# Query up-projection placed behind the scores and gating products, and the last weight slice's low part ahead of a unit's work, in a one-layer hybrid decoder

## The chip, the cores and the metric

The kernel runs on one core of one Trainium2 chip. The metric is the device time of one execution in microseconds (us); lower is better. Five engines work side by side and meet at semaphores: TensorE (PE for matmuls, PEld for its weight loads), VectorE (DVE), ScalarE (ACT), GpSimd (POOL) and SyncE (SP, which issues most DMAs here).

## What is computed

One decoder layer over 1024 positions of width 1024, float32. Three sub-layers, each `x <- LayerNorm(alpha * x + f(x))`: a hybrid token mixer, a cross-attention into 256 memory tokens, and a mixture of 16 experts. The change touches only the front of the mixer:

```python
rq, rk, rv, rg, su, sv, cq, ckv, kr = jnp.split(x @ w_in, split_points, axis=-1)
rq, rk = apply_rope(rq), apply_rope(rk)              # retention, 4 heads of 64
ret = head_group_norm(retention_chunkwise(rq, rk, rv))
ret = jax.nn.silu(rg) * ret
sgu = spatial_gating(su, layer_norm(sv), sgu_w, sgu_b)   # per 128 positions
q  = (rms_norm(cq, q_norm_g) @ w_uq)                 # 256 -> 8 heads of 64 + 32
kv = (rms_norm(ckv, kv_norm_g) @ w_ukv)              # 128 -> 8 heads of 64 + 64
```

In the chunkwise retention each chunk of 128 positions needs its own scores (keys times queries, times a decay mask), a product of the queries with a running state, and an update of that state by the chunk's keys and values.

## The kernel before

The program is a row of phases with a barrier between them: `project`, `prepare`, `attend`, `mix_out`, `cross_attend`, `experts`, `overflow`. Within a phase each engine runs its own instruction list in the order in which the code is written; nothing reorders it across engines.

**`project`** computes `x @ w_in` in 32 units: four column chunks (in the order QK, LAT, UV, VG) times eight token tiles of 128. For precision both operands are split into a high and a low part, so each of the eight slices (`KD`, 128 rows of the contraction) costs three matmuls (L261 high times high, L262 high times low weights, L263 low times high weights); a unit is 24 matmuls into one of four PSUM banks. The weights of a chunk are kept in eight slices: ACT copies the high part of a slice (`whi`, L212), DVE subtracts to get the low part (`wlo`, L293). The buffers are single, so a slice of the next chunk may be written only when PE is through with the old one: `slice_free` lets slices 0 to 6 go when the last unit of the chunk has used them, and slice 7 when that unit is summed. `next_slices` places the splits in the lists of ACT and DVE: seven before the last unit's own work, the eighth at the head of the following unit, thus behind the last unit's own work.

```python
            c = u // NT
            if u % NT == NT - 1 and c < 3:
                for s in range(KD - 1):
                    split_w(c + 1, s)
            elif c and u % NT == 0:
                split_w(c, KD - 1)
```

PE waits for `wlo` slice by slice in the first unit of a chunk. DVE's own work for a unit is, for UV units, the layer norm of `sv` (L379 to L386, with a round trip to POOL), for LAT units the rotated key and the scaled latents, for VG units one product `sg` (L390). `unit_taken` counts units whose bank DVE has finished with; PE reuses a bank four units later. When all 32 low slices are made, SP issues six loads for the next phase (`w_uq`, `w_ukv`, `sgu_wT` and three small ones, L198 to L203); DVE scales them in `prepare_weights` ahead of the fourth VG unit (L324 to L327).

**`prepare`** goes through eight token tiles. For tile t PE runs, in this order: the values (L511), the query up-projection (L516, 4 matmuls of 384 columns that show as 8 records, since a float32 matmul is two passes), the retention scores (L529), the gating products (L534), the retention output (L541, L543), the state update (L550), the transposes of the next tile's latents and retention inputs (L489 to L498), the keys (L557) and the transposes of the rotated queries (L562). The query up-projection waits for `qT_copied`, ACT's copies (L593) of the previous tile's transposed queries out of the same two banks (3 and 4). ACT copies the un-rotated part of the queries out (`q_tok`, L581); DVE decays the scores (L620), rotates the queries (L628 to L634), takes the norm statistics of the retention output (`bn_stats` L638, L641), makes the gated output (L645), updates the state (L654), normalises the retention output (L658, which increments `out_taken` and so frees bank 7 for the gating products of the next tile), multiplies by the gate (L662), and begins the next tile (L611, L616).

Of the kernel before, what the change touches and what calls it, by code (L numbers as in the profile page):

```python
# [15 lines left out]
P = 128  # L16
S, D = 1024, 1024
NT = S // P
KD = D // P
# [7 lines left out]
QR, KVR = 256, 128  # L27
# [68 lines left out]
def over(ap, shape):  # L96
    return ap.broadcast_to(shape)
# [6 lines left out]
def project(nc, k):  # L104
# [39 lines left out]
    unit_taken = k.sem("unit_taken")  # L144
# [7 lines left out]
    with nc.psum_tensor("unit_ps", [P, 4, 512], f32) as ps, \  # L152
# [12 lines left out]
        def next_slices(u, split_w):  # L165
# [8 lines that stand above are left out]
        @block.sync  # L174
        def _(sp):
            for c in range(4):
                for s in range(KD):
                    n = c * KD + s
                    if c == 0:
                        if s >= RAWX:  # L180
                            sp.wait_ge(x_late_lo_done, s - RAWX + 1)
                        sp.dma_start(xraw[:, s % RAWX, EARLY], A["xT"][s][:, EARLY]).then_inc(x_loaded[s % RAWX], 16)
                    if n >= RAWW:
                        sp.wait_ge(w_lo_done, n - RAWW + 1)
                    w = CHUNK_W[order[c]]
                    o = CHUNK_AT[order[c]]
                    sp.dma_start(wraw[:, s, 0:w], A["w_in"][s * P:(s + 1) * P, o:o + w]).then_inc(w_loaded[s], 16)
                    if c == 0:
                        sp.dma_start(xraw[:, s % RAWX, LATE], A["xT"][s][:, LATE]).then_inc(x_late_loaded[s % RAWX], 16)
                    if n == 2:  # L190
                        sp.dma_start(k.cst[:], A["cst"]).then_inc(small_loaded, 16)
                        sp.dma_start(posi[:], A["positions"]).then_inc(small_loaded, 16)
                if c == 0:
                    sp.dma_start(gsg[:], over(A["sgu_ln_g"], [P, SW])).then_inc(norm_loaded, 16)
                    sp.dma_start(bsg[:], over(A["sgu_ln_b"], [P, SW])).then_inc(norm_loaded, 16)

            sp.wait_ge(w_lo_done, 4 * KD)
            sp.dma_start(k.gq[:], A["q_norm_g"]).then_inc(k.up_loaded, 16)  # L198
            sp.dma_start(k.gkv[:], A["kv_norm_g"]).then_inc(k.up_loaded, 16)
            sp.dma_start(k.sgb[:], A["sgu_bT"]).then_inc(k.up_loaded, 16)  # L200
            sp.dma_start(k.wuq[:], A["w_uq"].rearrange("(k p) n -> p k n", p=P)).then_inc(k.up_loaded, 16)
            sp.dma_start(k.wukv[:], A["w_ukv"]).then_inc(k.up_loaded, 16)
            sp.dma_start(k.wsg[:], A["sgu_wT"]).then_inc(k.up_loaded, 16)  # L203
# [76 lines left out]
        def _(dve):  # L280
            chain = [0]

            def link(ins):

                chain[0] += 1
                ins.then_inc(dve_chain, 1)
                dve.wait_ge(dve_chain, chain[0])
# [58 lines left out]
            dve.wait_ge(norm_loaded, 32)  # L346
            for u, (c, t) in enumerate(units):
                b = u % BANKS
                next_slices(u, split_w)
                if u == 3 * NT + 3:  # L350
                    prepare_weights()
                dve.wait_ge(unit_summed, u + 1)
                if c == CH_QK:

                    x = ps[:, b, :].rearrange("p (g f) -> p g f", f=32)
                    cb, sb_ = over(k.cos[:, t:t + 1, 0:32], [P, 16, 32]), over(k.sin[:, t:t + 1, 0:32], [P, 16, 32])
                    a3, b3 = (z[:].rearrange("p (g f) -> p g f", f=32) for z in (ta, tb))
                    dve.tensor_tensor(a3, x, cb, ALU.mult)
                    dve.tensor_tensor(b3, x, sb_, ALU.mult).then_inc(unit_taken, 1)
                    dve.wait_ge(unit_taken, u + 1)  # L360
                    a4, b4, o4 = (z.rearrange("p (g i f) -> p g i f", i=2, f=32) for z in (ta[:], tb[:], k.qk[:, t, :]))
                    dve.tensor_tensor(o4[:, :, 0, :], a4[:, :, 0, :], b4[:, :, 1, :], ALU.subtract)
                    link(dve.tensor_tensor(o4[:, :, 1, :], b4[:, :, 0, :], a4[:, :, 1, :], ALU.add))
                elif c == CH_LAT:

                    x = ps[:, b, QR + KVR:QR + KVR + ROPE]
                    dve.wait_ge(act_part, 2 * t + 2)
                    dve.tensor_tensor(ta[:, 0:ROPE], x, k.cos[:, t, 32:64], ALU.mult)
                    link(dve.tensor_tensor(tb[:, 0:ROPE], x, k.sin[:, t, 32:64], ALU.mult))
                    dve.tensor_tensor(k.kr[:, t, 0:16], ta[:, 0:16], tb[:, 16:32], ALU.subtract)  # L370
                    link(dve.tensor_tensor(k.kr[:, t, 16:32], tb[:, 0:16], ta[:, 16:32], ALU.add))

                    dve.wait_ge(rstd_ready, t + 1)
                    dve.tensor_scalar(k.cq[:, t, :], ps[:, b, 0:QR], rs[:, 0:1], None, ALU.mult)
                    dve.tensor_scalar(k.ckv[:, t, :], ps[:, b, QR:QR + KVR], rs[:, 1:2], None, ALU.mult)\
                       .then_inc(unit_taken, 1)
                elif c == CH_UV:
                    dve.wait_ge(act_part, 2 * NT + t + 1)
                    link(dve.bn_stats(stat[:], ps[:, b, SW:2 * SW]))  # L379
                    dve.bn_aggr(mv[:], stat[:]).then_inc(var_ready, 1)  # L380
                    dve.wait_ge(rstd_ready, NT + t + 1)
                    dve.tensor_scalar(ta[:, 0:SW], ps[:, b, SW:2 * SW], mv[:, 0:1], rs[:, 0:1], ALU.subtract, ALU.mult)\
                       .then_inc(unit_taken, 1)
                    dve.wait_ge(unit_taken, u + 1)
                    link(dve.tensor_tensor(tb[:, 0:SW], ta[:, 0:SW], gsg[:], ALU.mult))
                    link(dve.tensor_tensor(k.sv[:, t, :], tb[:, 0:SW], bsg[:], ALU.add))  # L386
                else:

                    dve.wait_ge(act_part, 3 * NT + 2 * t + 2)
                    dve.scalar_tensor_tensor(k.sg[:, t, :], xraw[:, t % 2, 0:RW], 1.0, ps[:, b, RW:2 * RW], ALU.add, ALU.mult)\  # L390
                       .then_inc(unit_taken, 1)
# [31 lines left out]
def prepare(nc, k):  # L423
    at, A, cst = k.at, k.dram, k.cst
    lat = at("lat_T", 185, [P, 2, QR + KVR])
    qkt = at("qk_T", 188, [P, 2, 4 * P])
    wuq, wukv, wsg, sgb = k.wuq, k.wukv, k.wsg, k.sgb
# [15 lines left out]
    HD = 4 * MQ  # L443
# [5 lines left out]
    q_sum = k.sem("q_sum")  # L449
# [10 lines left out]
    qT_copied = k.sem("qT_copied")  # L460
# [11 lines left out]
    with nc.psum_tensor("banks2", [P, 8, 512], f32) as ps, \  # L472
# [12 lines left out]
        def _(pe):  # L485
# [17 lines left out]
            for t in range(NT):  # L503
                b = t % 2
# [4 lines left out]
                if t:  # L509
                    pe.wait_ge(v_copied, t)  # L510
                pe.matmul(ps[:, 2, :], lat[:, b, QR:QR + KVR], wukv[:, MW:2 * MW], start=True, stop=True).then_inc(v_sum, 1)  # L511
                if t:
                    pe.wait_ge(qT_copied, 2 * t)
                for j in range(2):
                    for s in range(QR // P):
                        last = pe.matmul(ps[:, 3 + j, 0:HD], lat[:, b, s * P:(s + 1) * P],  # L516
                                         wuq[:, s, j * HD:(j + 1) * HD], start=(s == 0), stop=(s == QR // P - 1))
                last.then_inc(q_sum, 1)

                pe.wait_ge(qk_copied, t + 1)  # L520
                if t:
                    pe.wait_ge(kn_copied, 2 * t)
# [1 line left out]
                for h in (0, 2, 1, 3):  # L524
# [4 lines left out]
                    last = pe.matmul(o, kk, q, start=True, stop=True)  # L529
# [3 lines left out]
                for g in range(SG):  # L533
                    pe.matmul(ps[:, 7, RW + g * SD:RW + (g + 1) * SD], wsg[:, g, :],  # L534
                              k.sv[:, t, g * SD:(g + 1) * SD], start=True, stop=True)


                pe.wait_ge(sc_decayed, t + 1)
                pe.wait_ge(qd_made, t + 1)
                for j in range(2):  # L540
                    pe.matmul(ps[:, 7, j * P:(j + 1) * P], qdt[:, j * P:(j + 1) * P], state[:, j, :], start=True, stop=False)  # L541
                    for h in (2 * j, 2 * j + 1):
                        last = pe.matmul(ps[:, 7, h * RD:(h + 1) * RD], sc[:, h, :], k.rv[:, t, h * RD:(h + 1) * RD],  # L543
                                         start=False, stop=(h == 2 * j + 1))
                last.then_inc(out_sum, 1)

                if t + 1 < NT:
                    pe.wait_ge(kd_made, t + 1)
                    for j in range(2):
                        last = pe.matmul(ps[:, 6, j * P:(j + 1) * P],  # L550
                                         kd[:, b, 2 * j:2 * j + 2, :].rearrange("p h d -> p (h d)"),
                                         k.rv[:, t, j * P:(j + 1) * P], start=True, stop=True)
# [3 lines left out]
                for j in range(4):  # L556
                    last = pe.matmul(ps[:, 5, j * P:(j + 1) * P], wukv[:, j * P:(j + 1) * P],  # L557
                                     lat[:, b, QR:QR + KVR], start=True, stop=True)
                last.then_inc(kn_sum, 1)
                pe.wait_ge(q_rotated, t + 1)  # L560
                for h in range(MH):
                    last = pe.transpose(ps[0:MQ, 3 + h // 4, (h % 4) * P:(h % 4 + 1) * P], qtok[:, b, h, :], ident)  # L562
# [1718 lines left out]
```

## Time and profile before

| | |
|---|---|
| median of 3 runs | 1021.8 us (1018.81 to 1023.63) |
| the profiled execution's own time | 1026.81 us |
| its span | 1025.0 us |
| PE busy | 977.7 us (95%) |
| DVE busy | 588.1 us (57%) |
| ACT busy | 350.2 us (34%) |
| POOL busy | 192.9 us (19%) |
| mean granted TensorE clock | 0.982 of full speed |

In the trace `project` ends at about 177 us, `prepare` runs from 178.7 to 265.4 us, and the attention phase follows. A row of a timeline gives the start, the duration, engine, line, operation and tiles; records of the same line that touch are merged ("x8"), and the bracket says how long the engine sat idle before it and what ended that. Durations of PE are modelled from issue to drain, so steps are best read from start to start.

### The profile page before, as it was taken

The page shows a single profiled execution, that of the slowest core. Times are in us where ns is not written, and L with a number is a line of the kernel's source. Part 1 is how long each engine was busy: PE and PEld are TensorE (multiplying, and loading weights), DVE is VectorE, ACT ScalarE, POOL GpSimd, SP SyncE. Part 2 cuts the span into 40 slices and gives each one's busy share as a digit, 9 for nine tenths or more (in the row PEclk, how much of TensorE's full clock was granted, in tenths as well). Part 3 has the DMA queues.
Part 4 walks back from the last instruction along what each step waited for, and adds up shares of the span by engine and source line. Part 5 has one row for each costly group of instructions (what it writes and reads, how often), then busy time and mean ns, then how long its engine had stood idle before and what let it go on. Part 6 is the DMA issues. An engine that isn't in the chain of part 4 may idle for free. (4 is left out here: it accounts for less than half of the span.)

```text
span 1025.0 us, 15739 instructions
## 1 busy us (share of the span) xinstructions
PE 977.7 (95%) x5687; PEld 840.0 (82%) x5687; DVE 588.1 (57%) x1255; ACT 350.2 (34%) x737; POOL 192.9 (19%) x262
## 2 busy tenths in 40 slices
PE   7999999999899999899999999999999999999994
PEld 6898877677778999888885888888878989897983
DVE  7734340677566666464456446448633476767675
ACT  6112131434365544340005242331223244434441
POOL 0022100112042110002220000002400134343444
PEclk9999999999999999999999999999989999999998
DMA  9122010000799200170022300032787888989872
GB/s 313 55 68 82 1 62 1 1 1 23 282 414 359 104 21 22 34 274 1 1 82 85 123 1 1 1 115 106 285 269 268 286 290 286 305 310 326 292 278 87
DMA packets 67277, 151.59 MB, mean 148 GB/s; under 512 B 8720, under 2 KB 16144, under 8 KB 67216
## 3 DMA queue, kind: packets, MB, share of 16 engines
q1 hardware_dynamic: 59920, 133.82, 37.2%
q0 software_dynamic: 7296, 16.95, 4.3%
q8 instruction: 39, 0.64, 0.2%
q14 instruction: 22, 0.18, 0.1%
HBM read 107.62 MB, written 52.03 MB: 156 GB/s over the span
## 5 line engine op out<-in xcount | busy, mean ns | idle before, releaser
L1873 PEld LDWEIGHTS h_ps<-xgT,e_gate_up 128*128 128x128 f32 x1024 | 153.9, 190 | 4.5 <-issue 2.2
L1873 PE MATMUL h_ps<-xgT,e_gate_up 128*128 128x176 f32 x1024 | 155.4, 313 | 2.2 <-DVEq L1966 2.2
L261 PE MATMUL unit_ps<-whi,xhi 128*128 128x512 f32 (+1 forms) x256 | 98.2, 383 | 8.3 <-DVE wlo L293 8.3
L262 PE MATMUL unit_ps<-wlo,xhi 128*128 128x512 f32 (+1 forms) x256 | 97.7, 381 | 0.0
L263 PE MATMUL unit_ps<-whi,xlo 128*128 128x512 f32 (+1 forms) x256 | 97.5, 381 | 0.0
L799 PEld LDWEIGHTS o_ps<-mla_v,prob_T 128*128 128x128 f32 x576 | 70.6, 194 | 10.6 <-issue 5.0
L799 PE MATMUL o_ps<-mla_v,prob_T 128*128 128x64 f32 x576 | 71.7, 275 | 5.1 <-ACT prob_T L864 5.0
L261 PEld LDWEIGHTS unit_ps<-whi,xhi 128*128 128x128 f32 x256 | 48.4, 189 | 16.8 <-DVE xlo L337 6.1
L1997 DVE SCALAR_TENSOR_TENSOR z<-y_ps,slot_weight,x_rows 128x512 f32<-128x512 f32 (+1 forms) x64 | 45.6, 746 | 27.2 <-PE y_ps L1887 24.8
L263 PEld LDWEIGHTS unit_ps<-whi,xlo 128*128 128x128 f32 x256 | 48.4, 189 | 7.7
L1885 PE MATMUL y_ps<-e_dn_hi,h_hi 128*128 128x512 f32 (+1 forms) x128 | 52.8, 412 | 1.9 <-DVE z L1997 1.9
L262 PEld LDWEIGHTS unit_ps<-wlo,xhi 128*128 128x128 f32 x256 | 48.5, 189 | 7.5
L1887 PE MATMUL y_ps<-e_dn_hi,h_lo 128*128 128x512 f32 (+1 forms) x128 | 50.9, 397 | 0.0
L1886 PE MATMUL y_ps<-e_dn_lo,h_hi 128*128 128x512 f32 (+1 forms) x128 | 50.8, 397 | 0.0
L1046 PE MATMUL mix_acc<-wo_hi,mixT_hi 128*128 128x512 f32 x128 | 50.6, 395 | 0.0
L1048 PE MATMUL mix_acc<-wo_hi,mixT_lo 128*128 128x512 f32 x128 | 49.9, 390 | 0.0
L1047 PE MATMUL mix_acc<-wo_lo,mixT_hi 128*128 128x512 f32 x128 | 49.8, 389 | 0.0
L855 ACT ACTIVATE prob<-s_ps,neg_max 128x640 f32<-128x640 f32 (+3 forms) x32 | 30.5, 954 | 56.2 <-issue 52.6
L925 DVE COPY prob_T<-t_ps 128x512 f32<-128x512 f32 (+3 forms) x48 | 29.9, 623 | 24.0 <-PE t_ps L786 23.9
L1982 DVE TENSOR_TENSOR h<-silu_g,h_ps 128x176 f32<-128x176 f32 x32 | 10.6, 332 | 55.4 <-ACT silu_g L1924 55.4
L1940 ACT ACTIVATE ln_junk<-z,z_neg_mean 128x1024 f32<-128x1024 f32 (+1 forms) x24 | 27.6, 1150 | 42.5 <-DVE z_neg_mean L2003 40.8
L1924 ACT ACTIVATE silu_g<-h_ps 128x176 f32<-128x176 f32 x32 | 10.1, 317 | 90.4 <-PE h_ps L1873 83.1
(323 smaller groups left out, 2092.1 us busy)
## 6 DMA issues: line engine op xcount, KB each, us to landing
e_gate_up<-w_gu SPq DMA_DIRECT2D x16, 2048.0 KB, 9.5
e_down_raw<-w_dn SPq DMA_DIRECT2D x16, 1024.0 KB, 5.8
slot_rows<-zeros SPq DMA_DIRECT2D x22, 522.0 KB, 6.3
slot_sums<-zeros SPq DMA_DIRECT2D x22, 512.0 KB, 6.3
x_rows<-slot_rows SPq DMA_DIRECT2D x16, 522.0 KB, 4.6
slot_sums<-z SPq DMA_DIRECT2D x16, 512.0 KB, 4.0
wraw<-w_in SPq DMA_DIRECT2D x24, 256.0 KB, 4.0
xraw<-xT SPq DMA_DIRECT2D x16, 256.0 KB, 4.9
```

Of the source, the lines that this page charges most:

```text
L261: pe.matmul(o, hi, whi[:, s, 0:w], start=(s == 0), stop=False)
L262: pe.matmul(o, hi, wlo[:, s, 0:w], start=False, stop=False)
L263: last = pe.matmul(o, lo, whi[:, s, 0:w], start=False, stop=(s == KD - 1))
L799: last = pe.matmul(ops[:, i % 2, h * MV:(h + 1) * MV], probT[:, u % 2, j, (m - a) * P:(m - a + 1) * P], k.v[:, m, h * MV:(h + 1) * MV], st ...
L1046: pe.matmul(o, hi, whi[:, s, c], start=(s == 0), stop=False)
L1047: pe.matmul(o, hi, wlo[:, s, c], start=False, stop=False)
L1048: last = pe.matmul(o, lo, whi[:, s, c], start=False, stop=(s == KD - 1))
L1873: end = pe.matmul(hps[:, m, gu * CAP:(gu + 1) * CAP], gate_up[:, b, s, w], xT[:, s, :], start=(s == 0), stop=(s == KD - 1))
L1885: pe.matmul(out, hi, dn_hi[:, b, w, :], start=(f == 0), stop=False)
L1886: pe.matmul(out, hi, dn_lo[:, b, w, :], start=False, stop=False)
L1887: return pe.matmul(out, lo, dn_hi[:, b, w, :], start=False, stop=(f == 1))
L1997: dve.scalar_tensor_tensor(z[c][:, f], yps[r, BANK[u], :], wgt[r, b, c:c + 1], rows[b][r, c, f], ALU.mult, ALU.add, accum_out=zsum[r, c, j ...
```

## The change

Two edits. In `project` DVE makes the low part of slice 7 right after it has seen the last unit of a chunk summed, ahead of that unit's own work (ACT's order is as before). Because all 32 low slices can then be made before DVE has read the old contents of two small buffers for the last time, SP also waits for the 25th `unit_taken` before it issues the six loads. In `prepare` the query up-projection of a tile moves behind the scores and the gating products.

```diff
@@ project, sync
             sp.wait_ge(w_lo_done, 4 * KD)
+            sp.wait_ge(unit_taken, 3 * NT + 1)
             sp.dma_start(k.gq[:], A["q_norm_g"]).then_inc(k.up_loaded, 16)
@@ project, vector
-                next_slices(u, split_w)
+                c_at = u // NT
+                if u % NT == NT - 1 and c_at < 3:
+                    for s in range(KD - 1):
+                        split_w(c_at + 1, s)
                 if u == 3 * NT + 3:
                     prepare_weights()
                 dve.wait_ge(unit_summed, u + 1)
+                if u % NT == NT - 1 and c_at < 3:
+                    split_w(c_at + 1, KD - 1)
@@ prepare, tensor
                 pe.matmul(ps[:, 2, :], lat[:, b, QR:QR + KVR], wukv[:, MW:2 * MW], start=True, stop=True).then_inc(v_sum, 1)
-                if t:
-                    pe.wait_ge(qT_copied, 2 * t)
-                for j in range(2):
-                    for s in range(QR // P):
-                        last = pe.matmul(ps[:, 3 + j, 0:HD], lat[:, b, s * P:(s + 1) * P],
-                                         wuq[:, s, j * HD:(j + 1) * HD], start=(s == 0), stop=(s == QR // P - 1))
-                last.then_inc(q_sum, 1)
-
                 pe.wait_ge(qk_copied, t + 1)
...
                 for g in range(SG):
                     pe.matmul(ps[:, 7, RW + g * SD:RW + (g + 1) * SD], wsg[:, g, :],
                               k.sv[:, t, g * SD:(g + 1) * SD], start=True, stop=True)
+
+                if t:
+                    pe.wait_ge(qT_copied, 2 * t)
+                for j in range(2):
+                    for s in range(QR // P):
+                        last = pe.matmul(ps[:, 3 + j, 0:HD], lat[:, b, s * P:(s + 1) * P],
+                                         wuq[:, s, j * HD:(j + 1) * HD], start=(s == 0), stop=(s == QR // P - 1))
+                last.then_inc(q_sum, 1)
```

How the lists change. First DVE in `project`, around the third chunk boundary (the last UV unit, then the first VG units), before:

```order
L293 TENSOR_TENSOR wlo<-wraw,whi 128x512 [waits w_hi_done] x6
L379 BN_STATS stat<-unit_ps 128x6 [waits act_part,unit_summed]
L380 BN_AGGR mv<-stat 128x2 [waits dve_chain]
L382 TENSOR_SCALAR rope_a<-unit_ps,mv,rs 128x256 [waits rstd_ready]
L385 TENSOR_TENSOR rope_b<-rope_a,sgu_g 128x256 [waits unit_taken]
L386 TENSOR_TENSOR sv<-rope_b,sgu_bb 128x256 [waits dve_chain]
L293 TENSOR_TENSOR wlo<-wraw,whi 128x512 [waits w_hi_done,dve_chain]
L390 SCALAR_TENSOR_TENSOR sg<-xraw,unit_ps 128x256 [waits act_part,unit_summed] x3
```

and with the change:

```order
L294 TENSOR_TENSOR wlo<-wraw,whi 128x512 [waits w_hi_done] x6
L294 TENSOR_TENSOR wlo<-wraw,whi 128x512 [waits w_hi_done,unit_summed]
L385 BN_STATS stat<-unit_ps 128x6 [waits act_part]
L386 BN_AGGR mv<-stat 128x2 [waits dve_chain]
L388 TENSOR_SCALAR rope_a<-unit_ps,mv,rs 128x256 [waits rstd_ready]
L391 TENSOR_TENSOR rope_b<-rope_a,sgu_g 128x256 [waits unit_taken]
L392 TENSOR_TENSOR sv<-rope_b,sgu_bb 128x256 [waits dve_chain]
L396 SCALAR_TENSOR_TENSOR sg<-xraw,unit_ps 128x256 [waits act_part,unit_summed,dve_chain]
```

The eighth `wlo` moved from behind the five instructions of the unit's norm to ahead of them.

Second PE in `prepare`, from the values of a middle tile to its retention output, before:

```order
L511 MATMUL banks<-w_ukv,lat_T 128x512 [waits v_copied,lat_copied]
L516 MATMUL banks<-w_uq,lat_T 128x384 [waits qT_copied]
L516 MATMUL banks<-w_uq,lat_T 128x384 x3
L529 MATMUL banks<-qk_T 128x128 [waits state_made,kn_copied,qk_copied]
L529 MATMUL banks<-qk_T 128x128 x3
L534 MATMUL banks<-sv,sgu_wT 128x64 [waits out_taken]
L534 MATMUL banks<-sv,sgu_wT 128x64 x3
L541 MATMUL banks<-ret_state,ret_qd 128x128 [waits qd_made,sc_decayed]
```

and with the change:

```order
L517 MATMUL banks<-w_ukv,lat_T 128x512 [waits v_copied,lat_copied]
L527 MATMUL banks<-qk_T 128x128 [waits state_made,kn_copied,qk_copied]
L527 MATMUL banks<-qk_T 128x128 x3
L532 MATMUL banks<-sv,sgu_wT 128x64 [waits out_taken]
L532 MATMUL banks<-sv,sgu_wT 128x64 x3
L539 MATMUL banks<-w_uq,lat_T 128x384 [waits qT_copied]
L539 MATMUL banks<-w_uq,lat_T 128x384 x3
L547 MATMUL banks<-ret_state,ret_qd 128x128 [waits qd_made,sc_decayed]
```

The up-projection, with its wait for `qT_copied`, moved behind the two groups with the waits for `state_made`, `kn_copied` and `out_taken`, and now stands directly ahead of the group that waits for `sc_decayed`.

## Rows read from the trace of the kernel before

**Rows 1.** Page, part 1: busy time, share of the span, instructions.

```profile
PE 977.7 (95%) x5687; PEld 840.0 (82%) x5687; DVE 588.1 (57%) x1255; ACT 350.2 (34%) x737; POOL 192.9 (19%) x262
```

**Rows 2.** Timeline, second chunk boundary: start us, us, engine, line, operation.

```profile
85.81 4.29 DVE L293 TENSOR_TENSOR wlo<-wraw,whi 128x512 fp32r<-128x512 f32 x7
...
91.21 0.39 PE L261 MATMUL unit_ps<-whi,xhi 128*128 128x512 f32 x1
...
92.70 0.50 PE L261 MATMUL unit_ps<-whi,xhi 128*128 128x512 f32 x1 [0.65 <-DVE wlo L293]
```

**Rows 3.** Timeline, third chunk boundary, PE, DVE and ACT.

```profile
130.05 4.30 DVE L293 TENSOR_TENSOR wlo<-wraw,whi 128x512 fp32r<-128x512 f32 x7
...
132.12 0.62 ACT L212 ACTIVATE whi<-wraw 128x512 fp32r<-128x512 f32 x1
...
135.04 0.39 PE L261 MATMUL unit_ps<-whi,xhi 128*128 128x512 f32 x1
...
135.72 0.39 PE L261 MATMUL unit_ps<-whi,xhi 128*128 128x512 f32 x1
...
138.13 0.50 PE L261 MATMUL unit_ps<-whi,xhi 128*128 128x512 f32 x1 [1.57 <-DVE wlo L293]
```

**Rows 4.** The loads for `prepare`: timeline rows, then the DMA view's median landing.

```profile
140.41 0.43 SPq L203 DMA_DIRECT2D sgu_wT<-sgu_wT  x1
...
141.32 0.42 DVE L390 SCALAR_TENSOR_TENSOR sg<-xraw,unit_ps 128x256 f32<-128x256 f32 x1 [3.24 <-ACT xraw L240]
...
151.14 1.14 DVE L324 TENSOR_SCALAR w_uq<-w_uq,q_norm_g 128x768 f32<-128x768 f32 x2
...
sgu_wT<-sgu_wT SPq DMA_DIRECT2D x1, 256.0 KB, 5.9
```

**Rows 5.** Waits of PE, 188 to 262 us (tiles 1 to 7 of `prepare`).

```profile
PE banks L516 <- ACT mla_qT L593: 4.7, 7, 0.7
```

**Rows 6.** Timeline of PE, one middle tile of `prepare` and the next one's start.

```profile
235.52 2.85 PE L516 MATMUL banks<-w_uq,lat_T 128*128 128x384 f32 x8 [0.67 <-ACT mla_qT L593]
238.29 0.72 PE L529 MATMUL banks<-qk_T 64*128 64x128 f32 x8
238.95 1.11 PE L534 MATMUL banks<-sv,sgu_wT 128*128 128x64 f32 x8
239.89 0.48 PE L541 MATMUL banks<-ret_state,ret_qd 128*128 128x128 f32 x2
...
246.10 1.24 PE L516 MATMUL banks<-w_uq,lat_T 128*128 128x384 f32 x3 [0.67 <-ACT mla_qT L593]
```

**Rows 7.** Timeline of ACT and DVE, the same tile.

```profile
238.40 0.60 ACT L581 ACTIVATE q_tok<-banks 128x512 f32<-128x512 f32 x1 [2.45 <-PE banks L516]
...
239.74 0.28 DVE L628 TENSOR_TENSOR mla_rope_a<-banks,cos 128x128 f32<-128x128 f32 x1
...
240.86 0.28 DVE L634 TENSOR_TENSOR q_tok<-mla_rope_b,mla_rope_a 128x128 f32<-128x128 f32 x1
...
241.47 0.62 DVE L638 BATCH_NORM_STATS2 ret_stat<-banks 128x6 f32<-128x64 f32 x4 [0.33 <-PE banks L543]
...
244.36 1.10 DVE L658 TENSOR_SCALAR ret_on<-banks,ret_mv,ret_rstd 128x64 f32<-128x64 f32 x4
```

**Rows 8.** Timeline, end of the last tile of `prepare`.

```profile
261.06 0.48 PE L541 MATMUL banks<-ret_state,ret_qd 128*128 128x128 f32 x2
...
264.46 0.69 DVE L666 TENSOR_SCALAR mla_qT<-banks 96x512 f32<-96x512 f32 x1
264.82 0.59 ACT L593 ACTIVATE mla_qT<-banks 96x512 f32<-96x512 f32 x1
```

**Rows 9.** Windows: stretch, its us, busy us of PE, PEld, DVE, ACT, POOL, then clock.

```profile
180.00:183.70 3.70, 3.64 (x6) 1.88 (x7) 1.59 (x2) 1.06 (x2) 0.00 (x0) 0.54 0.00 0
279.00:285.00 6.00, 6.00 (x23) 5.15 (x22) 2.87 (x6) 4.05 (x13) 0.00 (x0) 0.51 1.02 416
```

**Rows 10.** Line L516, weight loads: ns min/median/max, first and last start.

```profile
L516 PEld LDWEIGHTS banks<-w_uq,lat_T x64: 186/190/337, 181.0 to 258.7; 128*128 128x128 f32 x64
```

## The prediction, made before the changed kernel ran

> **What bounds the kernel now.** I read the page's busy times first: TensorE is busy 95% of the span, no other engine above 57% [rows 1]. So a change that adds or removes no instruction can pay only by taking idle time, or half-clock time, from TensorE. I then read which waits stop TensorE in the two phases that are touched, and the timeline around each.
>
> In `project` it stops at chunk boundaries for the last slice's low part. At the second boundary it stands 0.65 us and at the third 1.57 us, both times for DVE's `wlo` [rows 2, 3]. The first boundary shows no such wait. DVE makes slices 0 to 6 in one block, which ends at 90.10 and 134.35 us, then does the last unit's own work, and only then slice 7.
>
> In `prepare` TensorE stops once per tile, seven times 0.67 us, ahead of the query up-projection, for ACT's copy of the previous tile's queries [rows 5]. A tile takes 246.10 - 235.52 = 10.58 us from one up-projection to the next [rows 6]. Tiles 1 to 7 repeat this pattern.
>
> For every term I need the new order of events, so I read start to start.
>
> **The change, part by part.** *Slice 7 ahead of the unit's own work.* Normally one slice takes TensorE 135.72 - 135.04 = 0.68 us, from one L261 to the next. At the third boundary the step is 138.13 - 135.72 = 2.41, that is 1.73 too much, and the first matmul after the stop lasts 0.50 in place of 0.39, 0.11 more [rows 3]: 1.84 us. At the second it is 92.70 - 91.21 = 1.49, 0.81 too much, with the same 0.11 [rows 2]: 0.92. Sum 2.76 us. With the change DVE's eighth split follows the seven: 4.30 / 7 = 0.61 us more, ready at 134.96, where TensorE wants it at 135.72 + 0.68 = 136.40. At the second boundary it is ready at 90.71 against 91.89. Both have over 1 us to spare, and ACT's high part is there at 132.74 [rows 3]. So all of the 2.76 us goes, and nothing takes its place.
>
> What is pushed back: DVE's work for the last unit of three chunks, by 0.61 us. TensorE wants that bank four units later, and a unit is 8 x 0.68 = 5.4 us, so this costs nothing.
>
> *The added wait on SP.* Behind it stand six loads and nothing else until the next phase. Before, the loads start with the release that also restarts TensorE at 138.13, the last is issued at 140.84, 2.7 us later, and lands about 5.9 us after issue, at 146.7; DVE first uses them at 151.14 [rows 3, 4]. Now they start when DVE ends the first VG unit, 141.32 + 0.42 = 141.74, which the gain above brings to 138.98. The last is issued at 141.7 and lands at 147.6; DVE comes to it at 151.14 - 2.76 = 148.4. The spare falls from 4.4 to 0.8 us. If it is missed, DVE stands at the fourth VG unit, and TensorE notices only if that lasts past the start of the last unit, over 16 us later (three units). Cost nil; without that cover it would be the lateness itself.
>
> *The up-projection behind scores and gating.* The 0.67 us wait is for ACT's copies. With 238.29 - 235.52 = 2.77 us of up-projection replaced by 0.66 us of scores and 0.94 us of gating ahead of it [rows 6], TensorE comes to the wait 1.6 us later than before, some 0.9 us after the copies are done. The period of TensorE's own work is then 10.58 - 0.67 = 9.91 us.
>
> But the move closes a **ring** that was open before. Let C be the start of the retention output (L541). The up-projection now ends at C. ACT's `q_tok` starts 238.40 - 238.29 = 0.11 after that end and lasts 0.60; DVE picks up about 0.07 later; from the first rotation to the last start is 240.86 - 239.74 = 1.12, and the next DVE instruction follows 0.20 behind (about the step between these short ones). So the norm statistics start at C + 0.11 + 0.60 + 0.07 + 1.12 + 0.20 = C + 2.10. Before, they started at 241.47 - 239.89 = C + 1.58, held by TensorE. From the statistics to the end of the normalisation, which frees bank 7, is 244.36 + 1.10 - 241.47 = 3.99 [rows 7]. Then 0.06 of hand-over, 0.94 of gating, 2.77 of up-projection: the next C is at 2.10 + 3.99 + 0.06 + 0.94 + 2.77 = **9.86 us**. So the ring is as long as TensorE's own work, 9.91. I take 9.91: it saves 0.67 us in each of seven tiles, 4.7 us. The scores, decayed early now, no longer stop TensorE; DVE reaches them (L620) while the up-projection runs.
>
> The ring's bounds: where the 0.07 and 0.20 are each 0.15 more, the period is 10.16 and the seven tiles give 2.9 us. On the other side, TensorE's restart after the old wait also costs about the 0.1 us seen at the boundaries, so 0.77 per tile, 5.4 us.
>
> *The last tile.* DVE's statistics come 0.52 us later relative to C, and with them its half of the last copy of queries. It started at 264.46, C + 3.40, and lasts 0.69; now it ends at C + 4.61. ACT's half ends at 264.82 + 0.59, C + 4.35 as before [rows 8]. The phase ends with the later: 0.26 us lost.
>
> *The first tile* has no wait to lose. Its opening runs at clock 0.54, half speed, after the barrier [rows 9]. Up-projection matmuls leave this stretch and scores and gating products enter it. I take 0, since I see the long ones and the weight loads slow alike: the L516 loads take 190 ns and up to 337 in that stretch [rows 10]. The Trainium skill, "TensorE: Matmul & The Clock Gate", section on LDWEIGHTS, gives a weight load as columns over 1.2 whatever the clock; by that the short gating products would lose nothing in the slow stretch and the sum would be about 0.5 us better. The trace speaks against it.
>
> **Sum.** 2.76 + 4.7 - 0.3 = 7.2 us less. The profiled execution took 1026.8 us (span 1025.0), so it would take 1019.6. The median of the three runs stands 5.0 us below it, at 1021.8: **1014.6 us** predicted. The bounds of the terms give 5.4 to 7.9 us, 1013.9 to 1016.4. Later phases are bound by TensorE too and start from semaphores, so I expect them to shift as a block.
>
> **The rivals.** *A, the ring binds.* For: it equals TensorE's work within 0.05 us, and three of its hand-overs (0.07, 0.20, 0.06) are estimates. If rotation and statistics run slower beside TensorE's writes, the period comes to 10.3, the tiles give 2.0 and the whole 2.76 + 2.0 - 0.3 = 4.5: 1017.3 us. Against: all its pieces are durations of this trace.
>
> *B, slower than before.* The same ring, much longer: gating waits for `out_taken`, and the up-projection, `q_tok`, the rotation and the next `out_taken` all queue behind. It decides at a period of 10.58 + (2.76 - 0.26) / 7 = 10.94 us; from there the kernel is slower. That takes 1.1 us more than my rows give, such as the normalisation starting only after a full extra POOL round. At 11.5 us per tile, 0.92 is lost seven times, 6.4 us, and with the last tile's 0.3 lost and the 2.76 gained the kernel is 3.9 us slower, 1025.7 us. Against: no piece in the rows comes near that.
>
> *C, the clock.* In the attention phase there is a stretch of 6 us at clock 0.51 [rows 9], worth up to 3 us (half of it). A shifted phase may lose it or get another: 7.2 +- 3, 1011.6 or 1017.6 us. The three runs spread over 4.8 us, as such stretches would make them. The Trainium skill, the same page, its part on the clock gate, says that the activity check runs freely and that the same kernel shows different counts of slow matmuls from run to run; no run here shows the cause yet.
>
> *D, slice 7 buys nothing,* because TensorE stops for something else there. Only 4.4 us are left, 1017.4. Against: the wait is named, and the next slice need is far off.
>
> **How the numbers follow.** Forecast as summed 0.55, A 0.17, C 0.16 (half each way), B 0.05, D 0.04, nothing left of it all 0.03. A measurement of this kernel can tell about 0.5%, 5.1 us. The forecast lies 2 us beyond that, so its own noise puts about a sixth of it within; so do most of A and D, and half of C: faster 0.66, same 0.29, slower 0.05 (B, and disturbed clocks). The range reaches to the good end of C and, past A and D, to near the old lower runs: 1010.5 to 1019.0.
>
> **What would show it.** Right: no wait of L261 for `wlo` but the first of the kernel; the wait of the up-projection for `mla_qT` gone, in its place small waits (0 to 0.2 us) of the gating products for `ret_on`; a tile period of 9.8 to 10.0 us; `prepare` some 4.4 us shorter, ACT's wait for the up-projection longer, DVE's wait for scores gone. Wrong: a period above 10.2 with gating waiting for DVE (A, B), a wait at the chunk boundaries under another name (D), or half-clock stretches at other places (C). DVE idle at `prepare_weights` would show the loads late, harmless unless TensorE stops in the last unit.

## The result and the profile after

The changed kernel takes 1016.3 us (median of 10 runs, 1011.4 to 1022.4) beside 1022.2 us before (10 runs, 1018.6 to 1029.4): ratio 0.9938, 95% interval 0.9914 to 0.9963. By the ratio that is 6.3 us less, with an interval of 3.8 to 8.8 (the two medians stand 5.9 apart); the forecast was 7.2 less, 1014.6. The profiled execution has a span of 1020.6 us, 4.4 below the 1025.0 of the one before.

The page's busy times answer to [rows 1]: the same work in a shorter span.

```profile
PE 979.0 (96%) x5687; PEld 841.9 (82%) x5687; DVE 587.6 (58%) x1255; ACT 350.4 (34%) x737; POOL 191.1 (19%) x262
```

**The chunk boundaries** [rows 2, 3]. First what is left of TensorE's waits for `wlo` up to 370 us: one, the first of the kernel. Then the timeline of the third boundary.

```profile
PE unit_ps L262 <- DVE wlo L294: 6.1, 1, 6.1
```

```profile
129.98 4.91 DVE L294 TENSOR_TENSOR wlo<-wraw,whi 128x512 fp32r<-128x512 f32 x8
...
134.97 0.39 PE L262 MATMUL unit_ps<-whi,xhi 128*128 128x512 f32 x1
...
135.65 0.39 PE L262 MATMUL unit_ps<-whi,xhi 128*128 128x512 f32 x1
...
136.33 0.39 PE L262 MATMUL unit_ps<-whi,xhi 128*128 128x512 f32 x1
```

DVE's eight splits end at 134.89, and TensorE goes through the boundary in steps of 0.68 us, where the old one had 2.41.

**The loads** [rows 4]:

```profile
139.43 0.42 DVE L396 SCALAR_TENSOR_TENSOR sg<-xraw,unit_ps 128x256 f32<-128x256 f32 x1 [1.54 <-ACT xraw L241]
...
142.24 0.43 SPq L204 DMA_DIRECT2D sgu_wT<-sgu_wT  x1
...
149.19 1.14 DVE L325 TENSOR_SCALAR w_uq<-w_uq,q_norm_g 128x768 f32<-128x768 f32 x2
```

SP's last load starts 1.8 us later than before, and DVE's first use of the loads shows no idle time ahead of it: covered, as forecast.

**A middle tile of `prepare`** [rows 6, 7]. First TensorE, then ACT and DVE.

```profile
215.92 0.38 PE L547 MATMUL banks<-ret_state,ret_qd 128*128 128x128 f32 x2
...
220.35 1.02 PE L517 MATMUL banks<-w_ukv,lat_T 128*128 128x512 f32 x2
...
221.30 0.72 PE L527 MATMUL banks<-qk_T 64*128 64x128 f32 x8
...
222.12 1.10 PE L532 MATMUL banks<-sv,sgu_wT 128*128 128x64 f32 x8
...
223.06 2.80 PE L539 MATMUL banks<-w_uq,lat_T 128*128 128x384 f32 x8
...
225.70 0.38 PE L547 MATMUL banks<-ret_state,ret_qd 128*128 128x128 f32 x2
```

```profile
216.12 0.60 ACT L587 ACTIVATE q_tok<-banks 128x512 f32<-128x512 f32 x1 [3.43 <-PE banks L539]
...
216.75 0.29 DVE L634 TENSOR_TENSOR mla_rope_a<-banks,cos 128x128 f32<-128x128 f32 x1 [1.63 <-ACT q_tok L587]
...
217.88 0.28 DVE L640 TENSOR_TENSOR q_tok<-mla_rope_b,mla_rope_a 128x128 f32<-128x128 f32 x1
...
218.08 0.62 DVE L644 BATCH_NORM_STATS2 ret_stat<-banks 128x6 f32<-128x64 f32 x4
...
220.97 1.10 DVE L664 TENSOR_SCALAR ret_on<-banks,ret_mv,ret_rstd 128x64 f32<-128x64 f32 x4
```

The period is 9.78 us (225.70 - 215.92), 9.77 on average over seven tiles, against 10.59 before: 5.7 us saved in all. It closes through the ring of the forecast, where C is again the start of a retention output: retention output at C = 215.92, statistics at C + 2.16, normalisation ending 3.99 later at 222.07, gating at 222.12, up-projection 0.94 on, next C 2.64 on. 2.16 + 3.99 + 0.05 + 0.94 + 2.64 = 9.78. The scores-to-gating step is 222.12 - 221.30 = 0.82 us, 0.16 more than the 0.66 before. TensorE's matmul rows show no wait here, since the modelled end of the scores (222.02) covers nearly all of it. The view of the gating line does, on its weight loads, seven times (ns min/median/max, first and last start; then idle time, times):

```profile
L532 PEld LDWEIGHTS banks<-sv,sgu_wT x64: 186/192/333, 180.7 to 252.2; 128*128 128x128 f32 x64
L532 PE MATMUL banks<-sv,sgu_wT x64: 275/275/473, 180.7 to 252.3; 128*128 128x64 f32 x64
...
  DVE ret_on L664: 2.0, 7
```

**The end of `prepare`** [rows 8]:

```profile
255.01 0.39 PE L547 MATMUL banks<-ret_state,ret_qd 128*128 128x128 f32 x2
...
258.68 0.59 ACT L599 ACTIVATE mla_qT<-banks 96x512 f32<-96x512 f32 x1
258.67 1.02 POOL L695 TENSOR_TENSOR ret_rstd<-ret_var,ret_half 128x4 f32<-128x4 f32 x1
258.86 0.68 DVE L672 TENSOR_SCALAR mla_qT<-banks 96x512 f32<-96x512 f32 x1
260.06 0.72 PE L779 MATMUL s_ps<-mla_kT,mla_qT 96*128 96x128 f32 x4 [1.67 <-PEq L479]
```

DVE's copy ends at C + 4.53, behind ACT's. Behind both, by its row, ends POOL's last instruction, at 259.69 = C + 4.68, and attention starts 0.37 later, at C + 5.05 in place of 265.73 - 261.06 = 4.67: 0.38 us lost.

**The opening of `prepare`** [rows 9] is where this execution gave something back. Windows of the stretch, with the granted clock third from the end of a row:

```profile
176.80:180.00 3.20, 2.96 (x14) 1.56 (x16) 1.91 (x3) 1.37 (x3) 0.81 (x2) 0.79 0.00 0
180.00:183.70 3.70, 3.70 (x18) 3.04 (x17) 0.76 (x2) 0.26 (x1) 0.00 (x0) 0.50 0.00 0
183.70:186.60 2.90, 2.90 (x7) 1.58 (x6) 0.00 (x0) 0.00 (x0) 0.00 (x0) 0.69 0.00 0
```

Counting each window's shortfall from full clock twice, as half-speed time, gives 1.3 + 3.7 + 1.8 = 6.8 us at 1.2 GHz, where before had 3.4 (0.46 x 2 x 3.7). From the first transpose to the first retention output it took 186.60 - 176.81 = 9.79 us, before 186.96 - 178.76 = 8.20. So 1.6 us of the gain was missing here. Either the new order of the first tile makes the slow stretch longer (**theory W** below), or its length differs from execution to execution by chance (**theory R**).

### The profile page after: what moved, and what is told of

The parts are those of the page before. It is cut to its first block and busy times, and to the rows that moved or that the text cites. A ratio compares the mean times of both kernels' runs of the same rounds, so it can differ in the third digit from the quotient of the medians.

```text
span 1020.6 us, 15739 instructions
## 1 busy us (share of the span) xinstructions
PE 979.0 (96%) x5687; PEld 841.9 (82%) x5687; DVE 587.6 (58%) x1255; ACT 350.4 (34%) x737; POOL 191.1 (19%) x262
## 5 line engine op out<-in xcount | busy, mean ns | idle before, releaser
L805 PEld LDWEIGHTS o_ps<-mla_v,prob_T 128*128 128x128 f32 x576 | 69.9, 193 | 11.3 <-issue 6.1
```

Of the source, the lines that this page charges most:

```text
L805: last = pe.matmul(ops[:, i % 2, h * MV:(h + 1) * MV], probT[:, u % 2, j, (m - a) * P:(m - a + 1) * P], k.v[:, m, h * MV:(h + 1) * MV], st ...
```

## The experiments

In what follows **opening** is the time from the first transpose of `prepare` to the first retention output, **period** the mean of the seven steps from one retention output to the next, **tail** the time from the last one to the start of attention. All are start to start on TensorE. These, the span and the mean granted clock are of the one profiled execution; the ratio is of all runs. `after_again` is the changed kernel and `q_mid_again` the kernel `q_mid`, run again.

| kernel | opening | period | tail | span | mean clock | ratio to before (95%) |
|---|---|---|---|---|---|---|
| before | 8.20 | 10.59 | 4.67 | 1025.0 | 0.982 | 1 |
| changed | 9.79 | 9.77 | 5.05 | 1020.6 | 0.980 | 0.9938 (0.9914 to 0.9963) |
| slice_only | 6.50 | 10.59 | 4.67 | 1021.4 | 0.987 | 0.9986 (0.9964 to 1.0007) |
| q_only | 6.55 | 9.77 | 5.05 | 1013.9 | 0.992 | 0.9968 (0.9945 to 0.9992) |
| q_mid | 6.50 | 9.69 | 4.63 | 1013.8 | 0.991 | 0.9916 (0.9892 to 0.9939) |
| first_old | 6.50 | 9.76 | 5.05 | 1013.1 | 0.990 | 0.9901 (0.9878 to 0.9923) |
| after_again | 6.55 | 9.77 | 5.05 | 1017.6 | 0.985 | 0.9931 (0.9901 to 0.9961) |
| q_mid_again | 8.08 | 9.69 | 4.62 | 1009.7 | 0.990 | 0.9909 (0.9875 to 0.9943) |
| ring_after | 6.56 | 10.67 | 5.75 | 1019.1 | 0.989 | single run |
| ring_mid | 6.50 | 9.69 | 5.14 | 1008.9 | 0.991 | single run |
| late_loads | 6.56 | 9.77 | 5.04 | 1019.3 | 0.985 | single run |

**slice_only: the first edit alone.** The changed `project`, and `prepare` with the block put back:

```diff
@@ prepare, tensor (changed kernel)
+                if t:
+                    pe.wait_ge(qT_copied, 2 * t)
+                for j in range(2):
+                    for s in range(QR // P):
+                        last = pe.matmul(ps[:, 3 + j, 0:HD], lat[:, b, s * P:(s + 1) * P],
+                                         wuq[:, s, j * HD:(j + 1) * HD], start=(s == 0), stop=(s == QR // P - 1))
+                last.then_inc(q_sum, 1)
                 pe.wait_ge(qk_copied, t + 1)
...
                               k.sv[:, t, g * SD:(g + 1) * SD], start=True, stop=True)
-                if t:
-                    pe.wait_ge(qT_copied, 2 * t)
...
-                last.then_inc(q_sum, 1)
```

> Only the first edit (slice 7's low part ahead of the last unit's own work, with SP's added wait); prepare as before. If the two edits add up: no wait for wlo at the chunk boundaries, project shorter by 2.8 us beside before apart from its first ten us, tile period in prepare 10.58 us, whole kernel 2.8 us below before (ratio about 0.997). If slice 7 buys nothing (its wait comes back elsewhere), the ratio is 1.000 and TensorE stops in prepare or at the boundaries under another name. First tile of prepare has the old order: from the first transpose to the first retention output about 8.2 us, as before, if the old order is what keeps the half-clock stretch short.

The boundary waits are gone and the old wait is back:

```profile
PE unit_ps L262 <- DVE wlo L294: 6.0, 1, 6.0
PE banks L522 <- ACT mla_qT L599: 4.7, 7, 0.7
```

Across all traces `prepare` opens at 176.3 to 176.9 us in the nine executions with this edit and at 178.8 and 179.3 in the two without: 2.5 us between the means, with the kernel's uneven first 30 us in it. Counted from the first matmul of the second chunk, which leaves that out, it is 178.76 - 51.29 = 127.5 us in the kernel before and 176.90 - 52.32 = 124.6 here:

```profile
51.29 0.35 PE L261 MATMUL unit_ps<-whi,xhi 128*128 128x416 f32 x1
...
178.76 0.30 PE L489 MATMUL banks<-constants,cq 128*128 128x128 f32 x1 [1.56 <-PEq L153]
```

```profile
52.32 0.35 PE L262 MATMUL unit_ps<-whi,xhi 128*128 128x416 f32 x1
...
176.90 0.30 PE L495 MATMUL banks<-constants,cq 128*128 128x128 f32 x1 [1.54 <-PEq L153]
```

The same count gives 124.6 in all nine with the edit and 127.4 in `q_only`: 2.8 to 2.9 us, as forecast. The ratio, 0.9986, holds 0.9973 (2.8 us) and no change alike; the ratio alone does not show this edit, the traces do.

**q_only: the second edit alone.** The kernel before, with the block moved in `prepare`:

```diff
@@ project (changed kernel)
-            sp.wait_ge(unit_taken, 3 * NT + 1)
...
-                c_at = u // NT
...
+                next_slices(u, split_w)
...
-                if u % NT == NT - 1 and c_at < 3:
-                    split_w(c_at + 1, KD - 1)
```

> Only the second edit (up-projection behind scores and gating); project as before, with the waits of 0.65 and 1.57 us at the second and third boundary. Tile period 9.77 us, seven tiles 5.7 us less; 0.4 us lost at the end of prepare. Theory W (the new order of the first tile makes the half-clock stretch at the opening of prepare twice as long): from the first transpose to the first retention output 9.8 us, so 1.6 us lost, whole kernel 3.7 us below before. Theory R (that length is chance of the run): about 8.2 us here, whole kernel 5.3 us below before.

```profile
PE unit_ps L261 <- DVE wlo L293: 8.2, 3, 6.0
```

The period is the changed kernel's, and the opening is 6.55 us with TensorE at full clock: theory W, by which it would be 9.8 us whenever the new order runs, falls. The ratio decides nothing: 0.9968 is 3.3 us, and its interval (0.8 to 5.6 us) holds the 3.7 us of theory W and the 5.3 of theory R. The profiled execution took 1015.7 us at a mean clock of 0.992, 3.8 us below the median of its 12 runs (1019.6): how much one profile can flatter.

**q_mid: the up-projection between scores and gating.**

```diff
                 last.then_inc(sc_sum, 1)
+                if t:
+                    pe.wait_ge(qT_copied, 2 * t)
...
+                last.then_inc(q_sum, 1)
                 if t:
                     pe.wait_ge(out_taken, t)
                 for g in range(SG):
...
-                if t:
-                    pe.wait_ge(qT_copied, 2 * t)
...
-                last.then_inc(q_sum, 1)
```

> Both edits, but the up-projection stands between the scores and the gating products, so that it no longer waits behind out_taken. Ring theory (gating waits for DVE's normalisation, and the up-projection behind it closes a ring of 9.77 us): the ring opens, the period falls to TensorE's own work, 9.6 to 9.7 us, the norm statistics are held by TensorE again, and the last tile loses nothing: 0.7 to 1.3 us below the changed kernel. Rival (TensorE's own work is already 9.77 us, the ring is only just met): period 9.77 to 9.8 us and no difference beyond the last tile's 0.3 us.

```profile
207.78 0.72 PE L527 MATMUL banks<-qk_T 64*128 64x128 f32 x8
...
208.51 2.85 PE L533 MATMUL banks<-w_uq,lat_T 128*128 128x384 f32 x8
...
211.20 1.00 PE L539 MATMUL banks<-sv,sgu_wT 128*128 128x64 f32 x8
212.04 0.44 PE L547 MATMUL banks<-ret_state,ret_qd 128*128 128x128 f32 x2
```

The period is 9.69 and the tail 4.63: 0.6 + 0.4 = 1.0 us less than the changed kernel in the trace. The ring through the norm is open, but the up-projection is back at ACT's copies of the queries (L599), which end at 207.38 + 1.08 = 208.46, 0.05 before it starts; its step behind the scores is 0.73 where 0.66 was seen. So TensorE's own work is at most about 9.69 - 0.07 = 9.62 us. The changed kernel's period less its late gating gives the same, 9.78 - 0.16.

**first_old: tile 0 keeps the old order.**

```diff
+                def query():
+                    if t:
+                        pe.wait_ge(qT_copied, 2 * t)
...
+                    last.then_inc(q_sum, 1)
+
+                if t == 0:
+                    query()
                 pe.wait_ge(qk_copied, t + 1)
...
+                if t:
+                    query()
```

> The changed kernel, but tile 0 of prepare keeps the old order (up-projection right behind the values). Theory W: the half-clock stretch at the opening of prepare is 3.4 us long again in place of 6.9, the way from the first transpose to the first retention output is 8.2 us in place of 9.8, and the kernel is 1.2 to 1.6 us faster than the changed one. Theory R: the same length as in the changed kernel on average, no difference. Tile period 9.77 us in both.

Opening 6.50 us, no shorter than the 6.55 of `q_only` with the new first tile: nothing for the order of the first tile to explain. Its ratio, 0.9901 from 6 runs, is the lowest, but its interval still overlaps the changed kernel's, and its trace differs from the changed kernel's only at the first tile. Its six runs had the highest clock of the group, 0.990 on average (see **All runs at one clock** below).

**after_again and q_mid_again: the changed kernel and q_mid side by side,** both as they were.

> The changed kernel once more, beside the others of this call on one chip. Tile period 9.77 us again (it is set by durations and semaphores), attention starts 5.05 us after the last retention output. Theory R says that the opening of prepare differs from execution to execution (6.5, 8.2 or 9.8 us from first transpose to first retention output, clock at half for 0, 3.4 or 6.9 us); theory W says 9.8 us again. Ratio 0.992 to 0.995.

> The up-projection between scores and gating, a second time and beside the changed kernel. Tile period 9.69 us, attention 4.63 us after the last retention output: 0.6 + 0.4 = 1.0 us below the changed kernel in equal clock conditions, so a ratio 0.001 below that of the changed kernel, which may not stand out of the spread of the runs.

First transpose and first retention output of after_again:

```profile
176.28 0.30 PE L495 MATMUL banks<-constants,cq 128*128 128x128 f32 x1 [1.56 <-PEq L153]
...
182.83 0.38 PE L547 MATMUL banks<-ret_state,ret_qd 128*128 128x128 f32 x2
```

The same changed kernel now opens in 6.55 us, at full clock, in place of 9.79; q_mid in 8.08 in place of 6.50. So one and the same kernel opens either way: theory R. Of eleven profiled executions eight opened at full clock, two with one slow stretch, one with a stretch twice as long, and both orders of the first tile are among the fast ones. Whether the order shifts the chances a little, eleven executions cannot tell. The medians are 1015.5 and 1012.0 us beside 1021.1 before; but the intervals of the two ratios overlap, and the traces account for only 1.0 us of that difference.

**All runs at one clock.** The record has the mean granted clock of every run, and within each kernel the runs with a lower clock tend to be the longer ones (correlations of -0.6 to -0.9). slice_only, q_only, q_mid and first_old were run beside the kernel before on one chip, after_again and q_mid_again beside it on another: 100 runs in all. A straight line fitted through their times and clocks, with one slope for all and a level for each kernel and chip, gives 8.1 us (standard error 0.7) for each 0.01 of mean clock. What is then left between a kernel and the one before is an estimate of its gain at equal clock:

| kernel | gain at equal clock, us (standard error) | terms read from the traces, us |
|---|---|---|
| slice_only | 2.0 (0.6) | 2.8 |
| q_only | 4.7 (0.6) | 5.3 |
| changed (after_again) | 7.7 (0.8) | 8.1 |
| first_old | 8.6 (0.8) | 8.1 |
| q_mid | 9.6 (0.6) | 9.1 |
| q_mid_again | 8.9 (0.9) | 9.1 |

Each gain lies within one and a half standard errors of the terms, and the gains of the two edits taken singly add up to that of both within one. The fit takes the clock as something that happens to a run; that an edit itself shifts it a little is not excluded.

**ring_after and ring_mid: more DVE work between statistics and normalisation.** In both orders:

```diff
                 for g in range(SG):
-                    dve.scalar_tensor_tensor(k.mixA[:, t, RW + g * SD:RW + (g + 1) * SD], ps[:, 7, RW + g * SD:RW + (g + 1) * SD],
-                                             sgb[:, g:g + 1], k.su[:, t, g * SD:(g + 1) * SD], ALU.add, ALU.mult)
+                    last = dve.scalar_tensor_tensor(k.mixA[:, t, RW + g * SD:RW + (g + 1) * SD], ps[:, 7, RW + g * SD:RW + (g + 1) * SD],
+                                                    sgb[:, g:g + 1], k.su[:, t, g * SD:(g + 1) * SD], ALU.add, ALU.mult)
+                link(last)
+                for g in range(SG):
+                    dve.scalar_tensor_tensor(k.mixA[:, t, RW + g * SD:RW + (g + 1) * SD], ps[:, 7, RW + g * SD:RW + (g + 1) * SD],
+                                             sgb[:, g:g + 1], k.su[:, t, g * SD:(g + 1) * SD], ALU.add, ALU.mult)
```

> The changed kernel with DVE's four gated-output products of each tile done twice (the second time over the first, same values), which puts about 0.9 us of DVE work between the norm statistics and the normalisation that frees bank 7. Ring theory: in the changed order this work is inside the ring that sets the period, so all of it shows: period 9.77 + 0.9 = 10.6 to 10.7 us, with TensorE waiting at the gating products for ret_on. Rival (TensorE's own work sets 9.77 us and DVE has about 1.4 us to spare per tile): period at most 9.9 us.

> The same doubled DVE work in the order with the up-projection between scores and gating. Ring theory: there the normalisation has over 2 us to spare before the gating products want it, so the period stays 9.7 to 9.8 us (the state update is ready only just in time for the scores, so a tenth or so may show). Rival (any added DVE work in a tile shows, whatever the order): 10.6 us.

Waits and one tile of ring_after:

```profile
PE banks L527 <- DVE ret_state L664: 4.2, 7, 0.6
...
PE banks L532 <- DVE ret_on L668: 2.2, 7, 0.3
```

```profile
218.07 0.83 DVE L651 SCALAR_TENSOR_TENSOR mix_ret_sgu<-banks,sgu_bias,su 128x64 f32<-128x64 f32 x4
...
218.94 0.86 DVE L655 SCALAR_TENSOR_TENSOR mix_ret_sgu<-banks,sgu_bias,su 128x64 f32<-128x64 f32 x4
...
219.71 1.15 DVE L664 SCALAR_TENSOR_TENSOR ret_state<-ret_state,constants,banks 64x64 f32<-64x64 f32 x4
```

From the first product to the state update it is 1.64 us, 0.75 before the doubling (219.03 to 219.78 in the changed kernel): 0.89 added, and the period grows by 0.89 (10.67 - 9.77, both rounded). The state update is late by it too, and the scores wait for that; the gating products behind them wait once more, for the normalisation, so that is the wait that ends last and the ring still closes there. The same work in ring_mid adds nothing per tile: 9.69. Only its tail, where DVE's last copy stands behind the doubled products, grows by 0.5. Two retention outputs of its timeline:

```profile
202.14 0.44 PE L547 MATMUL banks<-ret_state,ret_qd 128*128 128x128 f32 x2
...
211.83 0.44 PE L547 MATMUL banks<-ret_state,ret_qd 128*128 128x128 f32 x2
```

So the ring exists, it sets the period of the changed order, and it is the place of the up-projection behind `out_taken` that closes it.

**late_loads: the loads two units later.**

```diff
-            sp.wait_ge(unit_taken, 3 * NT + 1)
+            sp.wait_ge(unit_taken, 3 * NT + 3)
```

> The changed kernel, but SP waits for the 27th unit_taken in place of the 25th, so the six loads start two units, about 9.4 us, later. If the added wait is covered as forecast: the last load lands some 8 us after DVE comes to prepare_weights ahead of the fourth VG unit, DVE stands there that long, its first product of that unit is as late, and TensorE shows no wait before the last unit (project ends at the same time, within 0.1 us of the changed kernel from the second boundary on). If the loads are on the path, project ends up to 8 us later.

Waits of DVE from 140 to 180 us:

```profile
DVE w_uq L325 <- DMA sgu_wT<-sgu_wT: 8.0, 1, 8.0
```

DVE stands 8.0 us, TensorE not at all: its only wait in `project` is the first one, and from the first matmul of the second chunk to the opening of `prepare` it is 124.6 us as in the others. So the added wait on SP costs nothing, and would cost nothing if it were 9.4 us longer. DVE went on 5.6 us after the last issue (157.41 - 151.80), so in the changed kernel the loads were ready at about 142.24 + 5.6 = 147.8, 1.3 us before DVE's 149.19, where the forecast had 0.8 to spare.

## Why the prediction was right, point by point

- **Slice 7, 2.76 us.** Right in mechanism and size, by the steps at the boundaries and the 2.8 to 2.9 us from the second chunk to `prepare`. The delay of DVE's own unit work showed nowhere in TensorE's waits.
- **The wait on SP, nil.** Right twice over: the loads came in time, and `late_loads` shows that TensorE does not notice when they come 8 us late for DVE.
- **The up-projection, 4.7 us.** Right in mechanism, too small by 1.0: seven times 0.81. The step that was mis-sized is the period of TensorE's own work, "10.58 - 0.67 = 9.91 us", made by taking the shown idle 0.67 from the period. That idle counts from a modelled end. Before, it was 235.52 - 233.83 = 1.69 us from the values to the up-projection:

```profile
233.83 1.02 PE L511 MATMUL banks<-w_ukv,lat_T 128*128 128x512 f32 x2
```

Without a wait the values take 0.95 us from start to start (220.35 to 221.30), so the wait had cost 0.74. The up-projection takes 2.64 to its successor where I used 2.77, the step to the scores, and the retention output's first step is 0.22 behind the up-projection where it was 0.32 behind the gating products. So 0.74 + 0.13 + 0.10 came off a tile and the ring's 0.16 went on: 0.81. TensorE's own work is thus about 9.62, the bound that q_mid gives.
- **The ring, 9.86 us.** It came out at 9.78, and it, not TensorE's work, is the limit. The part of rival A that says so was right, its price not: 0.16 us per tile in place of 0.4. Piece by piece: 2.16 for 2.10, 3.99 for 3.99, 0.94 for 0.94, 2.64 for 2.77.
- **The last tile, 0.26 us lost.** 0.38. DVE's copy ends about where forecast (C + 4.53 for 4.61), but it is not the last: the step left out is POOL's `ret_rstd`, which waits for the same statistics, came later with them (C + 4.11 before, C + 4.68 now) and overtook both copies. From the last of the three to attention it is 0.32 us before and 0.37 now. Rows on POOL are rough, but all five executions with the changed order in tiles 1 to 7 and without doubled products show the same (tails of 5.04 and 5.05), and in the other six, where POOL ends ahead of a copy, attention starts 0.31 to 0.33 behind the last copy.
- **The first tile, nil.** Right on average, though not in the profiled execution. The sentence on the weight loads can be checked there: the eight records of the gating products take 182.48 - 180.72 = 1.76 us at granted clock 0.50 and 0.94 at full, and their weight loads 333 ns at most against a median of 192. The Trainium skill, "TensorE: Matmul & The Clock Gate", section on LDWEIGHTS, has one formula for a weight load, its columns over 1.2 in ns, and no second one for the other clock. For 128 columns that makes, as an estimate, 107 ns. These float32 loads of 128 columns agree with it at neither clock, and their time changes with the clock.
- **Rival C, the clock,** was true beside the forecast. By the same count as above, before spent 2 x 0.018 x 1025 = 37 us of its profiled execution at 1.2 GHz and q_only 16, so between single executions it weighs more than the 3 us priced. The terms of the trace sum to 2.8 + 5.7 - 0.4 = 8.1 us; the ratio says 6.3, the profiled spans 4.4. Of those spans' missing 3.7 us, 1.6 are at the opening of `prepare` and 0.9 at the start of the kernel, where TensorE kept steps of 1.28 us per slice, twice the usual, up to about 11.3 us in place of 9.2; 1.2 us lie behind `prepare` and were not followed up. The ratio's missing 1.8 us are within its interval, and the runs at one clock come to 7.7. The Trainium skill, same page, part on the clock gate, says of a kernel's start that the count of slow matmuls differs from run to run. The two starts here agree, and the eleven openings of 6.5, 8.1 to 8.2 and 9.8 us show the same at a later phase.
- **Rivals B and D** did not occur: the period is far from 10.94 us, and the boundary waits are gone.
- **The sum, 7.2 us.** That it lies 0.9 us from the measured 6.3 is in part luck: the up-projection's term was 1.0 too small, and what the clock and the spread of the runs took from the ratio went the other way. At equal clock the forecast is 0.5 below the 7.7 found. Of the signs, `prepare` came out 3.7 us shorter in the trace (86.97 to 83.25) where 4.4 was forecast; the opening's 1.6 is in that. The 1014.6 us forecast for the kernel leaned on a median of 1021.8 for the one before, which came out at 1022.2 over ten runs.

## What to carry to other kernels

When a group of work is moved behind another group's wait, write down every chain that now passes through it, from its own output back to that wait: here a move that cured one stall closed a ring of 9.78 us over a TensorE that needs about 9.62, and one place further up does without it. Take the cost of a stall on TensorE from starts of matmuls, not from the idle time shown, and look at the weight loads' waits for what a modelled end hides. Where an edit is worth a few us of a thousand, count its pieces in the trace, treat the spans of single profiles as samples of the clock as well, and where each run's clock is on record compare at equal clock.

## What the runs showed of the hardware

After the same stop of TensorE of 1.5 to 1.6 us at the opening of `prepare`, the granted clock stayed at full, or was at half for 3.4 us or for 6.8. The changed kernel showed the first and the last of these, `q_mid` the first and the second. At half clock all of TensorE's work took about twice its time: the values 1.94 us from start to start in q_mid_again (clock 0.51) against 1.02 in after_again, the gating products 1.76 against 0.94, their weight loads 333 ns against 192. What decides between the three in one execution stays open; no run here separates it.

At the start of the kernel the steps were double too, 1.28 us per slice against 0.68, up to 9.2 us in the profile before and about 11.3 us in the changed one. The clock column shows 1.00 for these microseconds, so the mean clock of a profile does not count them.
